# Feed-forward, way down: from feature-major to token-major, with the output norm summed along rows

## The reference, cut to what matters

```python
x = x + 0.5 * rmsnorm_2(swiglu(rmsnorm_2(x, g[0]), w_in, w_out), g[1])

def rmsnorm_2(x, g):          # over the 1024 features of a token
    y = xf * lax.rsqrt(jnp.mean(xf * xf, axis=-1, keepdims=True) + RMS_EPS)
    return y * g
def swiglu(h, w_in, w_out):   # D_FF = 2816
    gu = h @ w_in
    return (silu(gu[..., :D_FF]) * gu[..., D_FF:]) @ w_out
```

## Time and profile before

| | us |
|---|---|
| median of 3 runs | 1996.78 |
| lowest, highest | 1995.46, 2007.18 |
| span of the profiled execution | 1997.9 |

### The profile page before, as it was taken

One profiled execution on the slowest core, in us unless ns is written; L12 is line 12 of the kernel. 1 busy time (PEld: TensorE's weight loads), 2 busy tenths in 40 slices (PEclk: granted clock), 3 DMA queues, 4 the chain that ended last, 5 costly groups with the idle time before them and its releaser, 6 DMA issues.

```text
span 1997.9 us, 31359 instructions
## 1 busy us (share of the span) xinstructions
PE 1878.1 (94%) x12914; PEld 1665.4 (83%) x12914; DVE 1354.4 (68%) x1795; ACT 1103.4 (55%) x1625; POOL 10.3 (1%) x12
## 2 busy tenths in 40 slices
PE   7998999999999998999899899997999969899997
PEld 5887677777777777999788799997999958799997
DVE  3625999999999995655433465556677685265655
ACT  3334889888888985434333444445543362344444
POOL 0000000000000000000000000000000020000000
PEclk9999999999999999999999999999999978899998
DMA  6325899999999993554233354433598311455420
GB/s 250 127 87 202 327 369 367 349 370 351 369 364 365 361 369 142 188 190 148 78 110 129 158 195 176 176 134 127 191 93 280 113 44 48 176 195 189 174 92 21
DMA packets 56483, 409.41 MB, mean 205 GB/s; under 512 B 15360, under 2 KB 20992, under 8 KB 22160
## 3 DMA queue, kind: packets, MB, share of 16 engines
q1 hardware_dynamic: 51792, 400.51, 55.6%
q10 hardware_dynamic: 4544, 6.85, 1.1%
HBM read 406.22 MB, written 1.11 MB: 204 GB/s over the span
## 4 chain that ended last, share of the span: by engine, by line
PE 70%; DVE 25%; ACT 2%; issue 1%; DMA 0%; DVEq 0%; ACTq 0%; SPq 0%
PE wk L1589 26%; DVE ws_moe L1069 16%; PE acc L1567 13%; PE wk L378 5%; PE wk L1023 3%; PE wk L1908 3%; PE wk L384 2%; PE wk L1723 2%; PE wk L947 2%; PE acc L913 2%; PE wk L333 2%; PE acc L730 1%; PE acc L1937 1%; DVE rstd L305 1%; DVE sq L1136 1%
## 5 line engine op out<-in xcount | busy, mean ns | idle before, releaser
L1069 DVE TENSOR_TENSOR ws_moe<-ring,ws_moe 128x1024 fp32r<-128x1024 f32 x384 | 447.4, 1214 | 5.6 <-ACT ws_moe L1062 5.4
L1062 ACT ACTIVATE ws_moe<-ring 128x1024 fp32r<-128x1024 f32 x384 | 384.3, 1051 | 5.3 <-PE wk L1023 2.2
L1589 PE MATMUL wk<-hx,gu 128*128 128x256 f32 x2112 | 277.4, 290 | 4.8 <-DVE hx L1605 4.5
L1589 PEld LDWEIGHTS wk<-hx,gu 128*128 128x128 f32 x2112 | 266.0, 195 | 10.2 <-DVE hx L1605 6.7
L1023 PE MATMUL wk<-ws_moe,xp_moe 128*128 128x512 f32 x1024 | 269.5, 405 | 1.6 <-DVE xp_moe L1091 1.6
L1567 PE MATMUL acc<-hh_ffn,dn_ffn 128*128 128x256 f32 x2112 | 268.7, 284 | 2.0 <-issue 2.0
L1567 PEld LDWEIGHTS acc<-hh_ffn,dn_ffn 128*128 128x128 f32 x2112 | 261.0, 193 | 2.1 <-issue 2.1
L1589 PE MATMUL wk<-hx,gu_ffn 128*128 128x256 f32 x2112 | 260.6, 283 | 0.0
L1589 PEld LDWEIGHTS wk<-hx,gu_ffn 128*128 128x128 f32 x2112 | 256.6, 192 | 0.0
L1537 ACT ACTIVATE hT<-hT 128x256 f32<-128x256 f32 x88 | 36.8, 418 | 368.0 <-DVE hT L1622 368.0
L1023 PEld LDWEIGHTS wk<-ws_moe,xp_moe 128*128 128x128 f32 x1024 | 187.9, 189 | 43.8 <-issue 2.8
(11 more groups left out here) (355 smaller groups left out, 2356.4 us busy)
## 6 DMA issues: line engine op xcount, KB each, us to landing
ring<-in_u_moe SPq DMA_DIRECT2D x129, 1536.0 KB, 8.3
ring<-in_u_ffn SPq DMA_DIRECT2D x88, 1536.0 KB, 6.5
ring<-in_u_qkv SPq DMA_DIRECT2D x12, 1024.0 KB, 4.9
ring<-in_u_ple SPq DMA_DIRECT2D x8, 1280.0 KB, 5.6
ring<-in_u_in SPq DMA_DIRECT2D x9, 1024.0 KB, 4.8
ring<-in_u_glu SPq DMA_DIRECT2D x8, 1024.0 KB, 5.0
ring<-in_u_out SPq DMA_DIRECT2D x4, 1024.0 KB, 4.8
ring<-in_u_o SPq DMA_DIRECT2D x4, 1024.0 KB, 4.9
```

The costliest lines, as they stand in the source:

```text
L1062: e.activation(WS[:, n % NWS, 0, :], piece(x), ACT.Copy).then_inc(s.m_hi, 1)
L1069: e.tensor_tensor(WS[:, n % NWS, 1, :], piece(x), WS[:, n % NWS, 0, :].bitcast(F32), SUB).then_inc(s.m_lo, 1)
L1589: m = e.matmul(b[:, a * T:(a + 1) * T], gu_of(c, f)[:, x, a * 1024 + k * 128:a * 1024 + (k + 1) * 128], HX[:, y, k, :], start=k == 0 and a ...
```

## The change

It has three parts, in each of the four feed-forward parts.

1. The way down is turned round. `HH` is the stationary operand (128 hidden features by 128 tokens) and the down weights move, 512 columns wide: 12 products in place of 24. `acc` then holds tokens on the partitions: banks 0 and 1 tokens 0 to 127 with features 0 to 511 and 512 to 1023, banks 2 and 3 the same for tokens 128 to 255.
2. The sum of squares of a token lies along a row. ACT squares a bank with `accum_out` into one column of `fs` (the table of the root is loaded before), DVE adds two columns, ACT takes the root of one column, DVE inverts it. DVE copies each bank to `hT` and makes a 128 x 128 matrix with 0.5 times the inverse roots on its diagonal. PE multiplies `hT`, 128 x 128 at a time, by it: that both scales each token and turns the result back to feature-major, into the four `wk` banks. DVE multiplies by the gain and adds to `xT` in one instruction.
3. For c = 1 and c = 3 the split of the gate's first weights moves from behind the last pass to ahead of that pass's Silu on ACT and of its scaling on DVE.

```diff
--- before
+++ after
@@ -1470,8 +1470,7 @@
             K.then(("norm", ("ffn", c)), *[("u", c, f) for f in range(NF)])
             for f in range(NF):
                 load(("ffn", c, f), A["u_ffn"][c * NF + f], UNIT, (s.f_dl, c * NF + f + 1))
-            norms.then(("ffn_out", c))
-            K.then(("norm", ("ffn_out", c)))
+            K.then(*[("yt", c, j) for j in range(4)])
 
         def ffn_g(c):
             a = ((c // 2) * 8 + 4 * (c % 2)) * 8
@@ -1530,6 +1529,9 @@
                 n = c * NF + f
                 if 0 < f < NF - 1:
                     ffn_split_hi(e, c, f + 1, False)
+                if f == NF - 1 and c % 2:
+                    e.wait_ge(s.filled, K("u", c, NF - 2) + 1)
+                    ple_split_hi(e, c // 2, 0)
                 if f == 2 and c % 2:
                     e.dma_start(ple_tiles[c // 2][0], A["pT"][c // 2].rearrange("(k p) t -> p k t", p=128)).then_inc(s.ld_p, 16)
                 G_, U_, S_ = (hT[:, 3 * (f % 2) + i, :] for i in range(3))
@@ -1543,14 +1545,18 @@
                     ffn_split_hi(e, c, f + 1, True)
                 if c == 2:
                     factors_act(e, f)
-            if c % 2:
-
-                e.wait_ge(s.filled, K("u", c, NF - 2) + 1)
-                ple_split_hi(e, c // 2, 0)
             if c == 2:
 
                 e.wait_ge(s.eB, 6)
-            add_act(e, ("ffn_out", c), acc3, g_out, lambda j: e.wait_ge(s.f_end, 4 * c + j + 1))
+            e.activation(tiny[:, :], cs("eps"), ACT.Sqrt)
+            for i in range(4):
+                e.wait_ge(s.f_end, 4 * c + i + 1)
+                e.activation(sq[:, 2 * (i % 2):2 * (i % 2) + 2, :], pair(acc[:, i, :]), ACT.Square,
+                             accum_out=fs[:, i:i + 1]).then_inc(s.f_yq, 1)
+                if i % 2:
+                    e.wait_ge(s.f_ys, 2 * c + i // 2 + 1)
+                    e.activation(fs[:, 6 + i // 2:7 + i // 2], fs[:, 4 + i // 2:5 + i // 2], ACT.Sqrt, bias=cs("eps"),
+                                 scale=1.0 / D).then_inc(s.f_yr, 1)
 
         def ffn_pe(e, c):
             leave(e)
@@ -1562,11 +1568,11 @@
                 e.wait_ge(s.f_dl, n + 1)
                 if f == 0:
                     acc_in(e, ("ffn", c))
-                for d in range(8):
+                for d in range(4):
                     for i, (x, y) in enumerate(THREE):
-                        m = e.matmul(acc_tile(d), DN[:, f % 3, x, d * 128:(d + 1) * 128], HH[:, f % 2, y, :],
-                                     start=f == 0 and d % 2 == 0 and i == 0, stop=f == NF - 1 and i == 2, skip_group_check=True)
-                    if f == NF - 1 and d % 2:
+                        m = e.matmul(acc[:, d, :], HH[:, f % 2, y, d // 2 * 128:(d // 2 + 1) * 128],
+                                     DN[:, f % 3, x, d % 2 * 512:(d % 2 + 1) * 512], start=f == 0 and i == 0, stop=f == NF - 1 and i == 2)
+                    if f == NF - 1:
                         m.then_inc(s.f_end, 1)
                 if f < NF - 1:
                     m.then_inc(s.f_dn, 1)
@@ -1592,14 +1598,26 @@
                 if f:
                     down(f - 1)
             down(NF - 1)
-            sums_pe(e, ("ffn_out", c))
+            yt = [None] * 4
+            for q in range(2):
+                e.wait_ge(s.f_D, 2 * c + q + 1)
+                e.wait_ge(s.gk, 4 * g_at(("ffn_out", c)) + 2 * q + 2)
+                for j in range(4):
+                    if q == 0:
+                        yt[j] = bank_in(e, K("yt", c, j))
+                    for i in range(2):
+                        d = 2 * j + i
+                        m = e.matmul(yt[j][:, i * T + q * 128:i * T + (q + 1) * 128], hT[:, 4 * q + d // 2, d % 2 * 128:d % 2 * 128 + 128],
+                                     sq[:, 6, q * 128:(q + 1) * 128], start=q == 0 and i == 0, stop=q == 1, skip_group_check=True)
+                    if q:
+                        m.then_inc(s.filled, 1)
 
         def ffn_dve(e, c):
             leave(e)
             if c == 0:
                 ffn_early_dve(e, 0)
             _, DN, HH = ffn_area[c]
-            g, _ = ffn_g(c)
+            g, g_out = ffn_g(c)
             for k in range(8):
                 e.wait_ge(s.f_xh, 8 * c + k + 1)
                 e.scalar_tensor_tensor(out=HX[:, 1, k, :], in0=xT[:, k, :], scalar=g[:, k:k + 1], in1=HX[:, 0, k, :].bitcast(F32),
@@ -1615,6 +1633,8 @@
                     row, = inverse(e, ("ffn", c))
                 elif f + 1 < NF:
                     ffn_split_lo(e, c, f + 1, False)
+                elif c % 2:
+                    ple_split_lo(e, c // 2, 0)
                 G_, U_, S_ = (hT[:, 3 * (f % 2) + i, :] for i in range(3))
                 b = bank_out(e, k)
                 if f >= 2:
@@ -1630,9 +1650,29 @@
                     ffn_split_lo(e, c, f + 1, True)
                 if c == 2 and f >= 2:
                     next(more, None)
-            if c % 2:
-                ple_split_lo(e, c // 2, 0)
-            add_dve(e, ("ffn_out", c), 0.5)
+            for i in range(4):
+                q = i // 2
+                e.wait_ge(s.f_yq, 4 * c + i + 1)
+                if i % 2:
+                    e.tensor_tensor(fs[:, 4 + q:5 + q], fs[:, 2 * q:2 * q + 1], fs[:, 2 * q + 1:2 * q + 2], ADD).then_inc(s.f_ys, 1)
+                e.tensor_copy(hT[:, 2 * i:2 * i + 2, :], pair(acc[:, i, :])).then_inc(s.gk, 1)
+                if i % 2:
+                    e.wait_ge(s.f_yr, 2 * c + q + 1)
+                    r = fs[:, 6 + q:7 + q]
+                    e.reciprocal(r, r).then_inc(s.vec, V.up())
+                    e.wait_ge(s.vec, V.n)
+                    e.tensor_scalar(sq[:, 6, q * 128:(q + 1) * 128], cs("ident"), r, 0.5, MUL, MUL).then_inc(s.f_D, 1)
+            for j in range(4):
+                k = K("yt", c, j)
+                b = bank_out(e, k)
+                for i in range(2):
+                    d = 2 * j + i
+                    m = e.scalar_tensor_tensor(out=xT[:, d, :], in0=b[:, i * T:(i + 1) * T], scalar=g_out[:, d:d + 1], in1=xT[:, d, :],
+                                               op0=MUL, op1=ADD)
+                    if i == 0 and j:
+                        m.then_inc(freed[(k - 1) % 4], 1)
+                m.then_inc(s.x_new, 1)
+            e.memset(tiny[:, :], 0.0).then_inc(freed[k % 4], 1)
 
         def ffn_pool(e, c):
             leave(e)
```

More of the change, by code:

```diff
@@ L123 @@
     "m_last m_yl m_y m_gat m_xh m_xl m_gt m_G m_comb m_shift "
-    "f_gh f_gl f_dh f_dl f_xh f_xl f_xs f_g f_s f_p f_hh f_hl f_dn f_end "
+    "f_gh f_gl f_dh f_dl f_xh f_xl f_xs f_g f_s f_p f_hh f_hl f_dn f_end f_yq f_ys f_yr f_D "
     "x_hi x_lo w_hi w_lo ple_s ple_y "
@@ L163, in program @@
         tiny = sb("tiny", [128, 1])
+        fs = sb("fs", [128, 8])
         acc = ctx.enter_context(nc.psum_tensor("acc", [128, 4, 512], F32))
@@ L213, in program @@
         sq_at = Order()
-        sq_at.then("attn", "mem", "ffn", ("ffn_out", 0), "qkv", "o_out", ("ffn_out", 1), ("ple", 0), ("ple_out", 0), ("ffn_out", 2), "ssm", "z",
-                   ("ffn_out", 3), ("ple", 1), ("ple_out", 1))
+        sq_at.then("attn", "mem", "ffn", "qkv", "o_out", ("ple", 0), ("ple_out", 0), "ssm", "z", ("ple", 1), ("ple_out", 1))
         x_parts, w_parts = Tally(), Tally()
```

## The result

The changed kernel takes 1969.7 us (median of 4 runs, 1966.37 to 1971.03) for 1999.87 us before (4 runs). The ratio is 0.9847, 95% interval 0.9822 to 0.9872: 30.6 us, 1.5% faster. A second set of runs gave 1968.72 for 1999.66 us, ratio 0.9845 (0.9824 to 0.9867). The forecast was 1966, from 1958 to 1981.

The account below looks back on a forecast made before the run. PE was taken to bound the feed-forward passes, and a chain over ACT, DVE and PE the tails. Passes 12.1 us plus tails 18.7 make 30.8; 1996.8 - 30.8 = 1966 us, range 1958 to 1981.

Parts of the forecast that it names:

- The pass: Feed-forward way down on PE: 12 products at 0.228 us, 0.144 us less a pass, 12.1 us over 84 passes.
- The rule that speaks against the change: Trainium skill's issue gap, N / 2.4 + 2.5 ns a product: the wider products gain only 2.5 us in the 84 passes.
- the experts' 0.228 and 0.246: Steps of 512-wide products in the experts, steady piece and piece after a wait; 0.228 taken, 0.246 would give -6.0 us.
- DVE in the third part: Third feed-forward part: DVE's pass of 8.45 us hides under PE's 8.50 by 0.05 us.
- Rival 4: DVE limits the third part's passes; 1 us, inside the forecast's own range, no chance of its own.
- The tail up to `xT`: Chain from the start of `down(21)`: turn back at 3.5 us, last `xT` pair at 9.2, 5.3 us earlier.
- What is late next: First products using the new `xT`: attention 6.9 us earlier, state-space part 5.4, gate 3.2 twice; 18.7 us together.
- The moved split: Gate's split ahead of the last Silu costs nothing; otherwise DVE's 2.3 us would stand in the tail.
- Rival 1: PE at half clock in the tail: 3.6 us more a tail, 14.4 in all, 1980 us; chance 0.08.
- From span to time: Median of the runs taken as 1.1 us below the profiled span of 1997.9, so 1996.8 before the gain.
- The sum: Whole kernel: 12.1 us from the passes plus 18.7 from the tails, 30.8 us in all.

Follow-up runs that it names:

- `early_leave`: Changed kernel with PE's drain, the start of the next part's fence, moved from behind the turn back to ahead of it; 1969.58 us (one run).
- `late_split`: Changed kernel with the split of the gate's first weights put back behind the last pass, on ACT and DVE; 1978.18 us (one run).
- `late_turn`: Changed kernel with PE waiting for both diagonals before the turn back; 1983.17 us (one run).
- `narrow256`: Changed kernel with each 512-wide down product made as two of 256, operands and tail as changed; 1984.98 us (6 runs), ratio to before 0.9933.
- `late_table`: Changed kernel without the early activation that loads the root's table, so it loads ahead of the first one-column root; 1972.58 us (one run).

## Why the prediction was right, and where not

- *The pass.* 8.50 us was forecast from a step of 0.228, and 8.50 was measured (mean step 0.229): 11.2 us for 12.1 over the 84 passes. Most of the difference is the first pass of each part, where PE waits for DVE's split and gains nothing. The rule that speaks against the change (2.5 ns between the widths) would have given 2.5 us; the price of a product read here is 13 ns. The choice between the experts' 0.228 and 0.246 was right.
- *DVE in the third part.* 0.05 us of room was forecast, and it sufficed: 175.7 us in all four parts. Rival 4 did not occur.
- *The tail up to `xT`.* First product of the turn back at 3.5 and last pair at 9.2 were forecast; 3.53 and 9.30 were measured.
- *What is late next.* Attention 6.9 forecast, 6.6 measured; state-space part 5.4 and 5.3; the gate 3.2 and 2.6, twice. Together 17.1 for 18.7. The mis-sized term is "now it is queued behind the turn back and starts at 7.1": the drain of the fence stood there at no price, and it costs 0.5 us (`early_leave`). That is 1.0 of the 1.6 us that the tails fall short. By the other profiles the state-space part gained 4.8 and attention 6.1 to 6.2.
- *The moved split.* "Costs nothing" held. What it saves was put at DVE's 2.3 us; it is 3.3 us a tail, half of it clock (`late_split`).
- *The clock.* Rival 1 did not occur in the turn back, and the reason given, the short idle time, fits: it does occur at 2.2 to 2.3 us (`late_turn`, `late_split`). But I looked only at the tails. Ahead of attention's first products PE idles 2.0 us as before, and there the clock now falls in most profiles; 1.7 us go there.
- *The stop* of 0.8 to 2.2 us and the half clock behind it was in the profile of before, and I took it for nothing. It is absent from every profile with 512-wide down products, which is worth 0.8 to 3.6 us in the third part; `narrow256` brings it back.
- *From span to time.* I set the median 1.1 us under the span; the executions with a profile take 1.8 us more than their span. The span forecast was 1997.9 - 30.8 = 1967.1, and the two profiles have 1964.6 and 1968.3. Most of the 3.7 us between 1966 and 1969.7 is this mistake in translation.
- *The sum.* The times gave 30.6 and 30.9 us for 30.8. The mechanism is the one forecast, but that it came so close is partly luck: the terms fell short by 2.5 us and the clock in attention cost 1.7, while the stop, which is no term of the sum, gave 0.8 to 3.6.

## What to carry to other kernels

Where a product stream bounds the kernel, take its step from start to start at each width that the trace has: here, for fp32r, the widest moving operand paid, and operands only 128 columns wide hit another floor. When a chain between stages is shortened, count PE's idle times in the new one; from 2 us on the clock was at stake here, and at 2.3 us it doubled the price of two of these edits. Throwaway products helped only where they stood in the last idle time ahead of the work. A drain or fence that costs nothing may stand under some wait, and comes out when that wait is removed.

## What was not expected of the hardware

- An fp32r product steps 0.120 us at 256 columns and 0.227 at 512, 13 to 14 ns above columns at 2.4 GHz, and 0.111 at 128. At 256 it made no difference whether the neighbour had the same stationary operand.
- After 0.58 us of idleness the clock stayed, and after 1.52 to 1.55 too (`late_table`). After 2.21 to 2.30 it was down in the turn back of all six tails of `late_turn` and `late_split` that had such a gap (5.46 and 5.47 us for 3.84 in the two shown). After 2.0 ahead of attention it fell in 6 of 13 profiles, in one of the changed kernel and not in the other.
- PE stopped for 0.8 to 4.8 us without a semaphore wait in five of five profiles with 256-wide down products, beside instruction packets of 3 to 6 us in place of 1, and in none of eight with 512-wide ones, some of which have such packets too.
